# Attention of four heads at a time laid among the products of its own panels, and two output panels in its tail

## What is computed

```python
q, k, v = split(h @ w_in)      # 16 heads of 64, q and k by RMS norm of each head
qc, kc, vc = split(hc @ w_in)  # the same for the 256 context tokens
# neighbourhood attention: 8 rows x 64 columns, a query sees all 8 rows
# and 16 columns around its own, and all 256 context keys
s_nb = einsum(q_row, k_rows) * scale + bias ; s_nb = where(mask, s_nb, NEG)
s_cx = einsum(q_row, k_ctx) * scale
p = softmax(concatenate([s_nb, s_cx], -1))
o = (einsum(p[..., :n], v_rows) + einsum(p[..., n:], v_ctx)) @ w_out
x = x + g1 * o                 # then norm and the feed-forward part
```

## Time and profile before

| what | value |
|---|---|
| median of three runs | 3948.61 us |
| profiled execution | 3953.41 us, span 3951.6 us |
| mean granted clock of PE | 0.96 |
| busy: PE | 3690.2 us, 93% |
| busy: DVE | 2085.7 us, 53% |
| busy: ACT | 1442.3 us, 36% |
| busy: POOL | 645.3 us, 16% |
| DMA | 339.01 MB, mean 86 GB/s |

### The profile page before, as it was taken

One profiled execution on the slowest core, in us unless ns is written; L12 is line 12 of the kernel. 1 busy time (PEld: TensorE's weight loads), 2 busy tenths in 40 slices (PEclk: granted clock), 3 DMA queues, 4 the chain that ended last, 5 costly groups with the idle time before them and its releaser, 6 DMA issues.

```text
span 3951.6 us, 50824 instructions
## 1 busy us (share of the span) xinstructions
PE 3690.2 (93%) x19794; PEld 2974.2 (75%) x19794; DVE 2085.7 (53%) x3730; ACT 1442.3 (36%) x2248; POOL 645.3 (16%) x651
## 2 busy tenths in 40 slices
PE   8889999999988999999999887999999979899999
PEld 6676677787766766777878765788888879777887
DVE  4646755766456366656664535355454252564333
ACT  3445643443133446424331325331112233552222
POOL 1110121212220011122122110113333122000000
PEclk9989999999989899999999897999999989999999
DMA  4111232323331111333233100112322111212222
GB/s 155 60 64 49 86 114 105 121 108 133 112 113 61 54 59 65 118 123 125 104 135 129 66 22 1 43 70 80 118 91 101 65 54 54 70 49 75 101 96 80
DMA packets 65808, 339.01 MB, mean 86 GB/s; under 512 B 6816, under 2 KB 8352, under 8 KB 39968
## 3 DMA queue, kind: packets, MB, share of 16 engines
q1 hardware_dynamic: 65568, 335.78, 23.6%
HBM read 327.36 MB, written 8.39 MB: 85 GB/s over the span
## 4 chain that ended last, share of the span: by engine, by line
PE 76%; DVE 13%; ACT 8%; issue 2%; POOL 1%; DMA 0%; DVEq 0%; ACTq 0%; POOLq 0%; SPq 0%
PE ps L1718 23%; PE ps L1720 22%; PE ps L1719 22%; DVE wl L1969 3%; PE ps L1707 3%; PE ps L1845 2%; ACT wh L1864 2%; PE ps L1727 2%; DVE tt L1977 1%; PE ps L1838 1%; DVE pb L2195 1%; DVE acc L1977 1%; DVE hl L1977 1%; ACT opb L1957 1%; DVE u L1969 1%
## 5 line engine op out<-in xcount | busy, mean ns | idle before, releaser
L1969 DVE TENSOR_TENSOR wl<-raw,wh 128x2048 fp32r<-128x2048 f32 (+2 forms) x275 | 554.9, 2018 | 402.9 <-ACT wh L1864 383.2
L1864 ACT ACTIVATE wh<-raw 128x2048 fp32r<-128x2048 f32 (+2 forms) x275 | 457.2, 1663 | 815.7 <-PE ps L1720 811.4
L1718 PE MATMUL ps<-hh,wh 128*128 128x512 f32 (+1 forms) x1248 | 449.3, 360 | 11.0 <-DVE hl L1977 9.4
L2218 POOL TENSOR_TENSOR lt<-lt,cs 128x1024 f32<-128x1024 f32 x96 | 188.2, 1960 | 1657.6 <-DVE acc L1977 1657.6
L1719 PE MATMUL ps<-hl,wh 128*128 128x512 f32 (+1 forms) x1248 | 444.8, 356 | 0.0
L1720 PE MATMUL ps<-hh,wl 128*128 128x512 f32 (+1 forms) x1248 | 444.8, 356 | 0.0
L1718 PE MATMUL ps<-xhb,wh 128*128 128x512 f32 x832 | 371.4, 446 | 13.6 <-DVE xlb L1969 10.9
L1719 PE MATMUL ps<-xlb,wh 128*128 128x512 f32 x832 | 338.2, 406 | 0.0
L1720 PE MATMUL ps<-xhb,wl 128*128 128x512 f32 x832 | 338.0, 406 | 0.0
L1718 PE MATMUL ps<-xha,wh 128*128 128x512 f32 x704 | 284.1, 404 | 14.6 <-DVE wl L1969 12.0
L1719 PE MATMUL ps<-xla,wh 128*128 128x512 f32 x704 | 281.6, 400 | 0.0
(11 more groups left out here) (264 smaller groups left out, 7323.3 us busy)
## 6 DMA issues: line engine op xcount, KB each, us to landing
raw<-in_wts SPq DMA_DIRECT2D x199, 1024.0 KB, 4.8
lt<-in_wts SPq DMA_DIRECT2D x110, 512.0 KB, 3.5
raw<-in_wts SPq DMA_DIRECT2D x44, 512.0 KB, 3.4
raw<-in_wts SPq DMA_DIRECT2D x28, 448.0 KB, 3.1
x_scratch<-xt SPq DMA_DIRECT2D x3, 2048.0 KB, 9.1
xt<-x_scratch SPq DMA_DIRECT2D x3, 2048.0 KB, 8.1
oe<-in_relb SPq DMA_DIRECT2D x16, 384.0 KB, 3.9
bt<-in_big SPq DMA_DIRECT2D x1, 2688.0 KB, 9.5
```

Source lines behind the costliest of these rows:

```text
L1718: T.matmul(u.out, u.sh, u.mh, start=u.first, stop=False)
L1864: A.activation(u.h, u.raw, ACT.Copy).then_inc(*act.inc())
L1969: V.tensor_tensor(o_, a, b, op).then_inc(*dve.inc())
L2218: G.tensor_tensor(o_, a, b, op).then_inc(*pool.inc())
```

## The change

The panels of queries, values and keys of four heads (two chunks) now follow one another, four times. While the panels of four heads are made, a generator carries out the items of the four heads before, called every three steps (rate 4). An item is spread over five calls: four transposes of the item three back; the values of the item four back; the other four transposes; scores of this item and weights of the one before; nothing. All products of these panels call `step`.

Banks: 0 to 2 hold tiles, 3 the transposes of `Heads`, 4 and 5 the scores of one item, 6 four transposes, 7 the values. Keys have three buffers of one chunk, values two of two chunks, and a panel that would overwrite one calls the generator until the item that reads it has been issued. `Heads.push` scales the tile before ahead of the squares of the new one.

To make room, `xx` is written to DRAM (2 MB) at the end of the layer before. Chunks 0 and 1 of it are read back after the last keys, and chunks 2 to 7 when the attention has ended. The last eight items run with one call a step among the first two output panels, whose four output chunks are held in four banks: contraction chunks 0 to 5 for the first two, then for the other two, then chunk 6 and chunk 7 for all. The additions to `xx` of these four follow; then come panels three and four. The two fences go. The query gain is multiplied by the score scale once (`GQ`) instead of through the root.

```diff
-    for q in range(12):
-        add((("oqkv", q), 1), 2048, lambda i, q=q: kcols(i["od_w_in_2"][0], np.arange(q * 256, q * 256 + 256)))
+    for g in range(4):
+        for part, c0 in (("oq", 0), ("ov", 2 * D), ("ok", D)):
+            c0 += g * 256
+            add(((part, g), 1), 2048, lambda i, c0=c0: kcols(i["od_w_in_2"][0], np.arange(c0, c0 + 256)))
...
+                u = add("residual", came=[b.w, *back], part=(by_column(b.ap), gate, by_row(XX[:, mc, :])) if grid else
...
+                    if tokens_done:
+                        tokens_done()
...
+            def put_by():
+                add("load", dst=xx_dram, src=XX[:, :, :].rearrange("p k n -> p (k n)"), sem=s_by, free=list(xr_t))
+
+            def bring_back(n, k0, k1, free):
+                add("load", dst=XX[:, k0:k1, :].rearrange("p k n -> p (k n)"), src=xx_dram[:, k0 * S:k1 * S], sem=s_back[n], free=free)
...
                 def push(self, b, t, tile, nh, g_row, rope, place_, query):
                     x = Rec(b=b, t=t, tile=tile, nh=nh, g=g_row, rope=rope, place=place_, n=self.n, query=query)
                     self.n += 1
+                    if self.row and "d" not in self.row[-1]:
+                        self.scale(self.row[-1])
                     self.squares(x)
                     self.row.append(x)
-                    if len(self.row) > 1:
-                        self.scale(self.row[-2])
                     if len(self.row) > 2:
                         self.turn(self.row.pop(0))
...
+                def advance(self):
+                    if self.row:
+                        if "d" not in self.row[-1]:
+                            self.scale(self.row[-1])
+                            if len(self.row) == 1:
+                                return
                         self.turn(self.row.pop(0))
...
+                    pt = [((2 * n + y) % len(PTB), 0) for y in range(2)] if each else [(n % len(PTB), 512 * y) for y in range(3)]
...
+                    def s2(parts=range(0, 2 * nk, 4)):
+                        if 0 in parts:
+                            z["t"] = []
...
+                KT = [buf(f"okt{i}", [P, 768], M0 + (34344, 33024, 8192)[i]) for i in range(3)]
+                QS = [buf(f"oq{i}", [P, 256], M0 + (8960, 13824)[i]) for i in range(2)]
+                UO = [buf(f"ou{i}", [P, 256], M0 + (14080, 33792, 34048)[i]) for i in range(3)]
+                PB = [buf(f"opb{i}", [P, 1024], M0 + 9216 + 1024 * i) for i in range(3)]
+                PTB = [buf(f"opt{i}", [P, 512], M0 + 12288 + 512 * i) for i in range(3)]
+                E = buf("oe", [P, 13, 256], M0 + 26624)
+                VV = [buf(f"ov{i}", [P, 6, 256], M0 + 29952 + 1536 * i) for i in range(2)]
...
+                HR, SA_ = Ring(banks[0:3]), banks[4:6]
+                hd = Heads(Ring(banks[3:4]), UO, QS, [[by], []])
...
+                made = stages(pairs, PB, PTB, Ring(SA_), Ring(banks[6:7]), [[by] for _ in PB], [[] for _ in PTB], True)
+
+                def run():
+                    n = len(made)
+                    for t in range(n + 4):
+                        while t < n and not (ready[t // 8] and v_ready[t // 8]):
+                            yield
+                        if 0 <= t - 3 < n:
+                            made[t - 3][2]([0])
+                        yield
+                        if 0 <= t - 4 < n:
+                            made[t - 4][3]()
+                            made[t - 4][4]()
+                        yield
+                        if 0 <= t - 3 < n:
+                            made[t - 3][2]([4])
+                        yield
+                        if t < n:
+                            made[t][0]()
+                        if 0 <= t - 1 < n:
+                            made[t - 1][1]()
+                        yield
+                        yield
+
...
+                def place_k(g, i, b2, t2):
+                    for y in range(2):
+                        c = 2 * g + y
+                        if c > 2:
+                            while scored_t[c - 3] is None:
+                                bg()
+                        t = evac(KT[c % 3][:, i * P:i * P + P], b2.ap[:, y * P:y * P + P], [t2], scale=Q("odk"),
+                                 free=[scored_t[c - 3]] if c > 2 else [by])
...
+                hook["rate"] = 4
+                for g in range(4):
+                    p = get((("oq", g), 1), 8)
+                    firsts = first_tiles(p) if g == 0 else []
+                    run_later(turns, force=True)
+                    if g == 0:
+                        hd.q_free[1] = [h_ks[1][7]]
+                    for i in range(4):
+                        b = firsts[i] if firsts else tile(p, i)
+                        if i == 3:
+                            p.done(b.w)
+                        hd.push(b, b.w, i, 4, None, False, lambda b2, t2, g=g, i=i: place_q(g, i, b2, t2), False)
+                    p = get((("ov", g), 1), 8)
+                    for i in range(6):
+                        b = tile(p, i)
+                        if i == 5:
+                            p.done(b.w)
+                        if g > 1:
+                            while values_t[2 * g - 3] is None:
+                                bg()
+                        v_t = evac(VV[g % 2][:, i, :], b.ap[:, 0:256], [b.w], free=[values_t[2 * g - 3]] if g > 1 else start)
...
+                while hd.row:
+                    hd.advance()
+                bring_back(0, 0, 2, [scored_t[5], now("dve")[0]])
+                FR = Ring(banks[0:6])
+                hook["rate"] = 12
+                ps_, bs = [], []
+                for q in range(2):
+                    ps_.append(get((("oo", q), 1), 8))
+                    bs += [FR.next(), FR.next()]
+
+                def through(k0, k1, n0, n1):
+                    for k in range(k0, k1):
+                        while o_ks[k] is None:
+                            bg()
+                        for n in range(n0, n1):
+                            p, b, m = ps_[n // 2], bs[n], n % 2
+                            b.w = dense(b.ap, p.h[:, k, m * P:m * P + P], p.l[:, k, m * P:m * P + P], OH[:, k, :], OL[:, k, :],
+                                        k == 0, k == 7, k == 7, [o_ks[k]], *((p.w, b.free) if k == 0 else ()))
+                            step()
+                through(0, 6, 0, 2)
+                through(0, 6, 2, 4)
+                through(6, 7, 0, 4)
+                finish_bg()
+                bring_back(1, 2, 8, now("pe", "act"))
+                SA_[1].free = SA_[0].free
+                through(7, 8, 0, 4)
+                for q, p in enumerate(ps_):
+                    p.done(bs[2 * q + 1].w)
+                for m, b in enumerate(bs):
+                    residual(b, m, 0, 1, 1, True, True, [(s_back[int(m > 1)], 16)])
```

More of the change, by code:

```diff
@@ L1502, in pair, with attend @@
                     return s1, norm_, s2, s3, s4
-                made = [pair(n, it) for n, it in enumerate(pairs)]
+                return [pair(n, it) for n, it in enumerate(pairs)]
+            def attend(pairs, PB, PTB, wide):
+                S2 = [Bank(ps[:, wide * i:wide * i + wide, :].rearrange("p a n -> p (a n)")) for i in range(4 // wide)]
+                for i, b in enumerate(S2):
+                    b.free = sum((banks[wide * i + a].free for a in range(wide)), [])
+                n_ = now()
+                made = stages(pairs, PB, PTB, Ring(S2), Ring(banks[4:6]), [list(n_) for _ in PB], [list(n_) for _ in PTB])
                 for x_ in range(len(made) + 5):
@@ L1639, in odd @@
-                w = fence()
-                OH = buf("oh", [P, 8, S], M0, F32R)
-                OL = buf("ol", [P, 8, S], M0 + 18432, F32R)
-                E = buf("oe", [P, 13, 256], M0 + 14336)
-                PB = [buf(f"opb{i}", [P, 1024], M0 + 22528 + 1024 * i) for i in range(4)]
-                PTB = [buf(f"opt{i}", [P, 1024], M0 + 32768 + 1024 * i) for i in range(2)]
-                s_e = [sem(f"s_e{i}") for i in range(4)]
-                e_free = [w] * 4
-                zero_t = POOL(add("zeros", bufs=(E[:, 12, :],)))
+                OH = buf("oh", [P, 8, S], M0 + 4096, F32R)
@@ L1651, in load_bias @@
                     add("load", dst=e_, src=relb[h], sem=s_e[h % 4], free=e_free[h % 4])
-                for h in range(4):
-                    load_bias(h)
-                o_ks, pairs = [None] * 8, []
+                pairs = []
                 for c in range(8):
@@ L1679, in odd @@
-                            v=[[V_[:, j, h * 64:h * 64 + 64] for V_, j in ((VX, i), (VX, (i + 1) % 4), (VC, 0), (VC, 1))]
-                               for h in (2 * c, 2 * c + 1)],
-                            v_t=[v_t], bank=banks[6 + c % 2], col=i * P, first=i == 0, last=i == 3, finish=finish))
-                attend(pairs, PB, PTB, 1)
-                fence()
-                for q in range(4):
-                    p = get((("oo", q), 1), 8)
-                    if q:
```

(32 more changed lines are left out.)

147 lines of the change are left out of this document (70 added, 77 removed).

## The result

The changed kernel takes 3971.54 us (median of four runs, 3970.50 to 3972.03); the kernel before takes 3949.08 us on the same chip (3948.22 to 3950.39). The ratio is 1.0056, with an interval of 1.0039 to 1.0074: 22.5 us slower, where 4.1 were forecast, and above the range. The profiled execution has a span of 3969.8 us, 18.2 above that of the kernel before, whose own profiled execution lay 4.8 above its median.

What follows compares the result with a forecast made beforehand. It took PE's stalls and attention latency, some 20 us, as what bounds the odd layer's mixer; its terms summed to 369.1 us against 365.0, 4.1 longer, put on the median 3948.6: 3952.7 us, range 3938 to 3966.

Steps and rivals of the forecast that it cites:

- That order costs 1 us once, at the first tiles: Odd layer's products: scaling before the next squares makes DVE wait for POOL's root between the first two tiles, 1 us.
- the six border stalls: PE's waits where two panels of the odd layer's products meet; claimed to go, 5.7 us.
- the finer evictions of keys: Odd layer's keys: two evictions for one, claimed to lie on an idle ACT and cost 0.
- Products and attention before the tail: Odd layer before the tail: products 183.9 us, attention items 71.3, value-panel waits 5.4, ACT and DVE 2.
- 4.35 idle: Start of the tail: PE waits 4.35 us for the last key tile's chain, with no product behind it.
- The forced calls at the value panels: Values of panels 2 and 3: the generator runs nine calls in a row, PE waiting 2 x 2.7 = 5.4 us.
- 2 for ACT and DVE: Under the products: slack runs out only where a weight split falls between scores and second transposes, 2 us in all.
- The rival in which the second transposes wait under the products: Before the tail: half of 24 items wait 1 us and each panel 0.5 more; +17, 3968 us; chance 0.23.
- 32 + 22.5 + 13.8 + 9.5 + 22.6: Tail: PE's attention work, two output panels, waits with clock, wait before panel three with clock, panels three and four, in us.
- 12.8 + 7.7: Tail: 12.8 us of waits on split chunks, single bank and drain; 7.7 idle between second and third output panel.
- Its third rival: Tail: gaps and transposes hold the clock low for 20 us of attention; +9, 3962 us; chance 0.08.
- its second rival: Slower, before the tail: second transposes wait through one bank and evictions behind exponentials; +17, 3968 us; chance 0.23.

Runs made afterwards that it cites:

- the first two experiments: Changed kernel with the even layer's heads in the old order: 3963.8 us; kernel before with the new order in both layers: 3957.5 us.
- each single cure: Changed kernel with one edit each: even layer's old order 3963.8 us; low part ahead of additions 3968.4; chunk 5 for all four outputs 3967.9; read in two 3969.7.
- the combined kernel: Changed kernel with even layer's old order, low parts ahead of additions, chunk 5 for all four outputs and read in two: 3956.6 us, ratio 1.0017.
- the kernel with the tail's start filled: The combined kernel with the first six output-product steps put ahead of the last keys' transposes: 3954.4 us, ratio 1.0010.
- that with chunk 5 for all four: Changed kernel with contraction chunks 0 to 4 for two outputs, then the other two, then chunk 5 for all four: 3967.9 us, ratio 1.0051.

## Why the prediction was wrong

It said 3952.7 us with 3938 to 3966 about it; 3971.5 came. By its own steps:

**The step that failed: the order in `Heads`.** The prediction priced it as "That order costs 1 us once, at the first tiles", and summed from 3198.8 us on, the odd layer. The even layer uses the same class, stands in no term of the sum, and pays 8.1 us (59.6 to 67.7), which the first two experiments show from both sides: the old order put back in the change takes its heads to 59.6 us and gives 7.7 in the median, the new one put into the kernel before takes them to 67.6. The price that it gave was true where a scale is short. The step was also credited with the six border stalls, 5.7 us. In the kernel before with the new order they did not go but changed their cause, from the low part ahead of the scale to POOL's root beside the low part. In the changed kernel PE waits at five borders for the eviction from the one bank of head transposes, which stands on ACT behind a high part or two exponentials; the prediction had ACT idle there and the finer evictions of keys (0.77 us in place of 0.47) at nothing.

**Products and attention before the tail.** The forecast was 262.6 us and 4.35 idle, 267.0, from the counterpart of 3198.8 to the first output matmul; it took 270.5 (3203.5 to 3474.0). The forced calls at the value panels waited 1.91 + 0.20 and 1.66 + 0.92 us, 4.7 where 5.4 stood. The borders still waited 0.40, 0.35, 1.54, 0.40 and 0.74, 3.4 us, against none at borders and 2 for ACT and DVE, 1.4 too much. Four transposes among products kept PE for 0.35 us (0.42 forecast), values 1.03 and scores 1.07 with some 0.1 behind each: as forecast. The remaining 3 us no row singles out. The rival in which the second transposes wait under the products did not happen: from 3240 us to the end of the keys PE waited only at the borders and at the value panels.

**The tail.** Forecast 102.1 us from the first output matmul (32 + 22.5 + 13.8 + 9.5 + 22.6, and the 1.7 at the low clock that it had put at the start); measured 108.1. The waits were 18.3 us, 1.3 and 6.2 for the single bank and `ol`, 3.8 for the drain and 7.0 for panel three, against 12.8 + 7.7 = 20.5: slightly too dear. What was missed is the clock. The five low stretches hold 3.40, 2.90, 5.67, 3.40 and 5.67 us of busy PE. At 0.50 one 128x512 matmul starts every 0.43 us (3547.71, 3548.14), at 1.00 every 0.23 (3549.20, 3549.43), so about half of it, 10.5 us, was lost, against 4.5 forecast (1.7 + 1 + 1.8). The forecast priced one low stretch at the start and a few tenths for the rest; in this trace both waits of 3 us on `ol` bring one of their own. Its third rival had this mechanism, at 9 us and a chance of 0.08. The rest, 2 us, is pace of PE: at the prices that the prediction used for the items before (1.23, 0.84 and 1.21) its eight, eleven and twelve come to 33.6, not 32.

In sum: 8.1 us in the even layer, 6.0 of clock, 1.4 at the borders and some 5 spread, against 3 of waits that came out cheaper: 17.6 us above the forecast by the stretches, 18.4 by the medians. That each single cure gave nearly what it removed, and the combined kernel 15 of the 22.5, shows that the loss is made of these pieces and not of one. For the clock's share there is one comparison of single executions: the kernel with the tail's start filled has the combined kernel's waits, one low stretch less, and 2.8 us less. That all of it would go if the waits went is only argued.

Two sums of the prediction do not come out as written, and the forecast uses neither: the stalls that the change makes (5.4, 2, 6.1, 13.8 and 9.5) are 36.8 us, not about 34, and the 17 us of its second rival on top of 3952.7 are 3969.7, not 3968.

**Where the expected gain went.** The attention does hide: the stretch to the first output matmul is 49.4 us shorter. But the tail is 62.9 longer. What stays exposed is that the last eight items have 32 short steps to hide in, and chunk by chunk they are on the path (scores, weights, transposes, values, split), each with a wait that ends in `ol`. From the layer's first transposes to the end of the output product PE's waits sum to 23.8 us in the kernel before and to 32.3 in the changed one, and the low stretches hold 13.2 us of busy PE before and 21.0 after, worth 6.6 and 10.5. These two differences, 8.5 and 3.9, are 12.4 of the 13.6 us by which the layer got longer.

## What to carry to other kernels

Before pricing an edit, list every caller of the helper it touches, and for each compare the new loop's length (here the sum, the root's latency and the scale) with the tile of PE that has to cover it: the same order that costs nothing with a scale of one instruction makes DVE the bound with one of eight. A wait of 3 us that moves can bring its own stretch at 1.2 GHz with it, so price it with both. A phase whose last items have nothing left to hide in gets its drain back whatever is interleaved before; count the exposed items first.

## What the hardware showed that I had not expected

**POOL's small root beside DVE's large low part.** In the changed kernel, at a border (timeline of DVE and POOL):

```profile
3207.01 2.29 DVE L2086 TENSOR_TENSOR wl<-raw,wh 128x2048 fp32r<-128x2048 f32 x1
...
3207.24 2.93 POOL L2336 TENSOR_TENSOR st<-st 128x4 f32<-128x4 f32 x1
...
3210.20 0.42 DVE L2086 TENSOR_TENSOR ou<-ps,st 128x256 f32<-128x256 f32 x1 [0.90 <-POOL st L2336]
```

The low part ends at 3209.30, the root at 3210.17, 0.87 us later, and alone it takes 1.01. That reads as a root that waits until DVE's instruction is through, not as one that runs slower throughout. In the other direction, at 3553 us: POOL's three additions of 1.29 and DVE's two low parts of 2.29, together 8.45 us of work, take 7.83 side by side, nearly what they would one behind the other. Taken singly they alternate: POOL's first addition ends at 3554.62 after 1.26, DVE's first low part, begun at 3553.78, ends at 3556.77 after 2.99, POOL's second at 3557.91 after 3.14, DVE's second at 3560.06 after 3.15. So 0.7 of the 7.00 us that PE waits for panel three is this. The Trainium skill ("SBUF — State Buffer", Who interferes with whom) says that a DVE instruction with two SBUF inputs contends with a GpSimd instruction that reads SBUF, and, of DVE's modes with two ports, that whoever issues first has the shared pair for the whole instruction. The trace agrees, by the rows above, in both directions; the prediction did not use it, and by it the root at a border comes late in the new order, which cost PE 0.55 us a border in the kernel before with that order, and nothing that shows in the changed one. For a small root ahead of a low part it is not borne out, for in the kernel before the low part beside a root that had begun 0.33 us earlier took its usual time (timeline of POOL and DVE, with the earlier trace rows):

```profile
3216.22 1.01 POOL L2218 TENSOR_TENSOR st<-st 128x4 f32<-128x4 f32 x1
...
3216.55 2.29 DVE L1969 TENSOR_TENSOR wl<-raw,wh 128x2048 fp32r<-128x2048 f32 x1
```

**The clock in the tail.** In the changed kernel's tail each low stretch began in or right behind a wait of PE of 3 us or more, but for that at 3545.5, in front of which lie waits of 0.78, 0.78, 0.78 and 1.48 and little but transposes and values. From 3410 to 3471, with items among products, the clock was 1.00 throughout. But such a wait does not always bring one: with the tail's start filled, PE waited 3.10 us up to 3490.79, and the clock stayed at 1.00. Of the eleven kernels that have the first value panel's wait (1.91 to 2.27 us, at 3337 in the changed kernel), eight show a low stretch behind it, and three, the changed one, that with chunk 5 for all four and that with the old order in both layers, show none. Why, and whether the transposes have a share in the one exception above, stays open.
